# Four steps of an ordered f32 kernel on one core moved, and unread transpositions at three places

## The reference

```
def memory_attention(q, mk, mv):
    s = einsum('bshd,bmhd->bhsm', q, mk) * HEAD_DIM ** -0.5
    p = softmax(s, axis=-1)
    return einsum('bhsm,bmhd->bshd', p, mv)
...
for l in range(2):
    if l == 1:
        kv = rmsnorm(h, kv_norm) @ w_kv
        k_shared = rmsnorm(kv[..., :256], k_norm)        # per head of 64; the sliding keys
        v_shared = kv[..., 256:]
    proj = rmsnorm(h, norm_mix[l]) @ w_in[l]
    main, mq = proj[..., :768], proj[..., 768:]
    ...
    mkv = rmsnorm(mem, mem_norm[l]) @ w_mem_kv[l]
    mk = rmsnorm(mkv[..., :256], mem_k_norm[l])          # per head; the memory keys
    mv = mkv[..., 256:]
    mem_out = memory_attention(rmsnorm(mq, mem_q_norm[l]), mk, mv)
    h = h + concat(main_out, mem_out) @ w_out[l]
    h = h + sq_relu_mlp(rmsnorm(h, norm_mlp[l]), w_up[l], w_down[l])
```

## Time and profile before

| what | value |
|---|---|
| runs, us | 985.48, 986.09, 991.14; median 986.09 |
| the profiled execution, us | 986.21 |
| its span, us | 984.4 |
| TensorE busy | 976.6 us, 99%, 8662 instructions |
| VectorE busy | 692.8 us, 70% |
| ScalarE busy | 538.2 us, 55% |
| granted clock of TensorE | 1.00 |
| DMA | 168.97 MB, mean 172 GB/s |
| chain that ended last | PE 80%, DVE 12%, ACT 5%, issue 2%, DMA 1% |

### The profile page before, as it was taken

One profiled execution on the slowest core, in us unless ns is written; L12 is line 12 of the kernel. 1 busy time (PEld: TensorE's weight loads), 2 busy tenths in 40 slices (PEclk: granted clock), 3 DMA queues, 4 the chain that ended last, 5 costly groups with the idle time before them and its releaser, 6 DMA issues.

```text
span 984.4 us, 20641 instructions
## 1 busy us (share of the span) xinstructions
PE 976.6 (99%) x8662; PEld 948.6 (96%) x8662; DVE 692.8 (70%) x854; ACT 538.2 (55%) x688; POOL 38.7 (4%) x28
## 2 busy tenths in 40 slices
PE   9999999999999999999999999999999999999998
PEld 6999999999999999999989999999999999999998
DVE  5687765557789888999977655557777856555553
ACT  5657545546665455567645543445657755344432
POOL 0045230000000000000000000000000000000000
PEclk9999999999999999999999999999999999999999
DMA  7743433334644665453442755555553226655551
GB/s 280 253 172 132 160 102 122 130 129 172 246 171 172 214 213 180 164 212 129 171 172 87 256 175 209 202 181 175 172 179 117 71 103 216 215 206 174 183 201 43
DMA packets 24977, 168.97 MB, mean 172 GB/s; under 512 B 2768, under 2 KB 3536, under 8 KB 4944
## 3 DMA queue, kind: packets, MB, share of 16 engines
q1 hardware_dynamic: 24336, 165.82, 47.9%
q10 hardware_dynamic: 576, 2.20, 0.7%
HBM read 166.96 MB, written 1.05 MB: 171 GB/s over the span
## 4 chain that ended last, share of the span: by engine, by line
PE 80%; DVE 12%; ACT 5%; issue 2%; DMA 1%; DVEq 0%; SPq 0%; ACTq 0%
PE G L617 9%; PE G L611 8%; PE G L612 8%; PE D L606 7%; PE D L604 7%; PE D L605 7%; PE G L604 6%; PE G L605 6%; PE G L606 6%; DVE wlo L1922 5%; ACT whi L1404 2%; PE M L604 2%; PE M L606 2%; PE M L605 2%; PE M L909 1%
## 5 line engine op out<-in xcount | busy, mean ns | idle before, releaser
L1922 DVE TENSOR_TENSOR wlo<-raw,whi 128x2048 fp32r<-128x2048 f32 x155 | 354.9, 2295 | 114.8 <-ACT whi L1404 114.7
L1404 ACT ACTIVATE whi<-raw 128x2048 fp32r<-128x2048 f32 x155 | 295.5, 1909 | 59.0 <-PE D L606 46.2
L611 PE MATMUL G<-xh,whi 128*128 128x256 f32 x736 | 178.2, 286 | 0.0
L604 PE MATMUL D<-hh,whi 128*128 128x256 f32 x624 | 172.2, 276 | 0.0
L605 PE MATMUL D<-hl,whi 128*128 128x256 f32 x624 | 172.2, 276 | 0.0
L606 PE MATMUL D<-hh,wlo 128*128 128x256 f32 x624 | 172.2, 276 | 0.0
L612 PE MATMUL G<-xl,whi 128*128 128x256 f32 x736 | 172.2, 278 | 0.0
L611 PEld LDWEIGHTS G<-xh,whi 128*128 128x128 f32 x736 | 138.5, 188 | 4.5 <-issue 3.2
L612 PEld LDWEIGHTS G<-xl,whi 128*128 128x128 f32 x736 | 138.5, 188 | 1.3 <-issue 1.2
L604 PE MATMUL G<-xh,whi 128*128 128x256 f32 x448 | 123.9, 276 | 0.3 <-DVE wlo L1922 0.2
L605 PE MATMUL G<-xl,whi 128*128 128x256 f32 x448 | 123.7, 276 | 0.0
(11 more groups left out here) (450 smaller groups left out, 1643.7 us busy)
## 6 DMA issues: line engine op xcount, KB each, us to landing
raw<-wall_dram SPq DMA_DIRECT2D x155, 1024.0 KB, 4.9
x<-x_dram SPq DMA_DIRECT2D x4, 256.0 KB, 5.3
mem<-mem_dram ACTq DMA_DIRECT2D x1, 1024.0 KB, 4.8
poolw<-pool_w_dram ACTq DMA_DIRECT2D x1, 768.0 KB, 6.4
out_dram<-x SPq DMA_DIRECT2D x3, 256.0 KB, 2.2
cst<-cst_dram SPq DMA_DIRECT2D x1, 448.0 KB, 12.2
lora<-lora_dram SPq DMA_DIRECT2D x1, 256.0 KB, 11.7
sgw<-sg_w_dram SPq DMA_DIRECT2D x1, 256.0 KB, 12.4
```

Source lines behind the costliest of these rows:

```text
L604: mm(out, w_h, hi, start=start, stop=False, skip_group_check=skip)
L611: mm(out, w_h, hi, start=start, stop=False, skip_group_check=True)
L1404: signal(fn(whi[:, pan.slot, 0:w], raw[:, pan.slot, 0:w], ACT.Copy), "w_hi")
L1922: signal(tt(wlo[:, pan.slot, 0:w], raw[:, pan.slot, 0:w], f32(whi[:, pan.slot, 0:w]), SUB), "w_lo")
```

## The change

Four steps of the table move, each for some of the engines.

- `hn` is cut in two on TensorE's side (`hn_sum`): for the memory keys of layer 0 the sum stands ahead of the panel in0q. `hn_square` 0 stands ahead of mkv0's second panel, which for ScalarE means ahead of the copy of mv.
- the refinement of rstd becomes a step of its own (`late_root`) and stands behind the row sums in layer 0.
- VectorE reads ks in `score_m` 1, between the maxima and their correction; `root_s` 0 stands behind `hn_square` 2.
- in pair 1 of the gated net, second half, `more` stands ahead of the tap copies and of hh.

Two unread transpositions are added in the first panel of `wo` and behind the last part of `pv_s`, and two replace the four small products behind `rw_gates`.

```diff
-    W += [("panel", mkv + 1), ("hn_square", 0)] + sums[3]
-    W += [("panel", PAN["in0q"]), ("hn", 0), ("ahead_lo", PAN["in0q"]), ("begin", m0), ("square_m", 0), ("root", 3), ("sum_m", 0), ("score_m", 0), ("turn_mv", 0), ("panel", m0),
+    W += [("hn_square", 0), ("panel", mkv + 1)] + sums[3]
+    W += [("hn_sum", 0), ("panel", PAN["in0q"]), ("hn", 0), ("ahead_lo", PAN["in0q"]), ("begin", m0), ("square_m", 0), ("root", 3), ("sum_m", 0), ("late_root", 3), ("score_m", 0), ("turn_mv", 0), ("panel", m0),
...
-          ("panel", q1), ("turn_mv", 1), ("hn", 1), ...
+          ("panel", q1), ("turn_mv", 1), ("hn_sum", 1), ("hn", 1), ...
-          ("panel", q1 + 1), ("square_s", 0), ("ahead", k1), ("begin", k1), ("score_m", 1), ("sum_s", 0), ("root_s", 0), ("panel", k1),
-          ("begin", k1 + 1), ("hn_square", 2), ("exp_m", 1), ("soft_m", 1), ("hn", 2), ...
+          ("panel", q1 + 1), ("square_s", 0), ("ahead", k1), ("begin", k1), ("score_m", 1), ("sum_s", 0), ("panel", k1),
+          ("begin", k1 + 1), ("hn_square", 2), ("root_s", 0), ("exp_m", 1), ("soft_m", 1), ("hn_sum", 2), ("hn", 2), ...
@@ first_panel, TensorE @@
+                if count == XLN["wo"] and u == 0:
+                    free("M0")
+                    unread_turns(M[0], 2)
                 pe.wait_ge(S("xl"), count - 3 + u)
@@ rw_gates, TensorE @@
-            unread_few()
+            unread_turns(M[0], 2)
@@ pv_s, TensorE @@
+            if g == 2:
+                free("D1")
+                unread_turns(DB[1], 2)
@@ ffn, ScalarE @@
+                        if js == 1 and u:
+                            more(pan, 3)
                         act.wait_ge(S(f"up_read{f}"), 2 * j + u + 1)
...
-                        if not (u and isinstance(j, int) and j == ni - 1):
+                        if not (u and isinstance(j, int) and j in (1, ni - 1)):
                             more(pan, 3)
@@ root, VectorE @@
+            if n != 3:
+                late_root(n)
+
+        def late_root(n):
             dve.wait_ge(S("rs"), n + 1)
             newton(rstd[:], M[1][:, 0, :], D, 1e-6, rtmp[:], ("rs_read", n + 1))
@@ panel and score_m, VectorE @@
-            elif name == "kv":
+            elif name == "kv" and i:
                 read(p)
...
             own(ins)
+            if l:
+                read(PAN["kv"])
             row_newton(l, 0)
```

More of the change, by code:

```diff
@@ L413, in build @@
     W += [("panel", PAN["mkv1"]), ("hn_square", 1), ("panel", PAN["mkv1"] + 1), ("root", 5), ("parts5b",),
-          ("panel", q1), ("turn_mv", 1), ("hn", 1), ("square_m", 1), ("ahead", q1 + 1), ("begin", q1 + 1), ("sum_m", 1),
-          ("panel", q1 + 1), ("square_s", 0), ("ahead", k1), ("begin", k1), ("score_m", 1), ("sum_s", 0), ("root_s", 0), ("panel", k1),
-          ("begin", k1 + 1), ("hn_square", 2), ("exp_m", 1), ("soft_m", 1), ("hn", 2), ("ahead", k1 + 1), ("panel", k1 + 1),
+          ("panel", q1), ("turn_mv", 1), ("hn_sum", 1), ("hn", 1), ("square_m", 1), ("ahead", q1 + 1), ("begin", q1 + 1), ("sum_m", 1),
+          ("panel", q1 + 1), ("square_s", 0), ("ahead", k1), ("begin", k1), ("score_m", 1), ("sum_s", 0), ("panel", k1),
+          ("begin", k1 + 1), ("hn_square", 2), ("root_s", 0), ("exp_m", 1), ("soft_m", 1), ("hn_sum", 2), ("hn", 2), ("ahead", k1 + 1), ("panel", k1 + 1),
           ("begin", q2), ("ahead", q2), ("turn_p", 1), ("panel", q2), ("square_s", 1), ("turn_v",), ("score_s", 0),
@@ L686, in first_two, with unread_turns @@
                 ins.then_inc(S("pe_panel"), 1)
-        def unread_turns(bank):
-            for i in range(4):
+        def unread_turns(bank, n=4):
+            for i in range(n):
                 nc.tensor.transpose(bank[:, i // 2, i % 2 * P:(i % 2 + 1) * P], ident, ident)
-        def unread_few():
-            for _ in range(4):
-                mm(M[0][0:32, 0, 0:32], xh[:, 0, 0:32], xh[:, 0, 32:64], skip_group_check=True)
         def early_start():
@@ L1039, in rw_gn2 @@
             free("M0")
-            for i in range(2):
-                nc.tensor.transpose(M[0][:, 0, i * P:(i + 1) * P], ident, ident)
+            unread_turns(M[0], 2)
             freed.update({"D0": ("sb_out", 4), "D1": ("sb_arg", 4), "D2": ("rw_y", 1), "D3": ("rw_rs_read", 1)})
@@ L1361, in _ @@
                   "sg_turn": sg_turn, "sg_mix": sg_mix, "sb_turn": sb_turn, "sb_z": sb_z, "sb_q": sb_q,
-                  "sb_o": sb_o, "ffn": ffn, "mem_sum": mem_sum, "hn": hn, "turn_mv": turn_mv,
+                  "sb_o": sb_o, "ffn": ffn, "mem_sum": mem_sum, "hn_sum": hn, "turn_mv": turn_mv,
                   "turn_v": turn_v, "score_m": score_m, "turn_p": turn_p, "pv_m": pv_m, "pool_mm": pool_mm,
@@ L2567, in _ @@
         dve.wait_ge(S("ld_cst"), 16)
-        walk(dve, {"norm": norm, "root": root, "final_norm": final_norm, "pool": windows, "add_sq": add_sq, "add_mem": add_mem, "parts": parts, "parts5b": parts5b,
+        walk(dve, {"norm": norm, "root": root, "late_root": late_root, "final_norm": final_norm, "pool": windows, "add_sq": add_sq, "add_mem": add_mem, "parts": parts, "parts5b": parts5b,
                    "panel": panel, "rw_low": rw_low, "rw_gates": rw_gates, "rw_cum": rw_cum, "rw_key": rw_key, "rw_square": rw_square, "rw_scale": rw_scale,
```

## The result

The changed kernel takes 996.88 us (median of 6, 994.09 to 998.68) against 986.73 (6 runs) before: ratio 1.0102, interval [1.0083, 1.0120], slower by 10 us. The forecast was 988.4, the range ended at 991.4. The profiled execution took 994.09, the lowest of the six, with a span of 990.6 against 984.4, so the profile shows 6.2 us of the loss; the rest has to be found in other executions.

The account below looks back on a forecast made before the run. TensorE, busy 976.6 of 984.4 us, was taken to bound the kernel. 986.21 + 3.7 - 0.4 - 0.3 - 0.3 - 0.35 = 988.56, less 0.12, gave 988.4 us, range 986.6 to 991.4.

Parts of the forecast that it names:

- The pause: TensorE ahead of the early memory keys' sum: a new wait of 3.54 us, ended by ScalarE's squares; both edits there cost +3.7.
- hy began right behind mq: ScalarE at the memory keys: hy follows the copy of mq without waiting for the sum, 3.6 to 3.8 us later.
- The part that was to come back inside in0q: Panel in0q behind the memory keys' sum: waits inside it absorb 0.24 to 0.44 us of the lateness.
- The row sums: TensorE at 478.97: its 0.57 us wait goes, but TensorE waits for ml at wout0 instead; rival that the gain holds, 0.13.
- The sliding keys': TensorE at 740.65: the 0.57 us wait goes, part ends in a later VectorE wait; taken as -0.4 us.
- The clock: Rival, chance 0.15: TensorE's clock falls in the new wait, making in0q slower, for 990.8 or 993.1 us.
- the forecast's own sign of being wrong: Behind the memory keys' wait: the forecast is wrong if the granted clock falls there.
- the lower price: Clock rival with the first half of in0q at the slow rate: 2.35 us added, 990.8 us; rival's chance 0.15.
- The split of the gated stage: TensorE's wait at 303.58 for VectorE's split of a weight panel: earlier whi removes it, -0.3 us, bounds -0.41 and 0.
- The transpositions: Unread ones at rw_gates (-0.3), after the last sliding output (-0.35) and wo (0), quickening matmul pitch; rival of none, 0.08.
- the dearer case: At rw_gates: the stretch turns quick, gaining 0.58 us, but the next turns slow and loses the same; upper bound +0.63.
- The last place: Transpositions after the last output of the sliding attention: quicker matmuls behind, -0.35 us, bounds -0.35 and +0.14.

Follow-up runs that it names:

- e10: The change with the gated net's split edit taken back and ScalarE squaring the memory keys ahead of a split, shortening the pause: 989.25 us, ratio 1.0036.
- e12: The kernel before with the edit at the row sums alone: 986.94 us, ratio 1.0003.
- e11: The kernel before with the edit at the sliding keys alone: 986.01 us, ratio 0.9996.
- e9: The change without its edit at the gated net's split, memory keys' pause kept: 994.71 us, ratio 1.0076.
- e1: The change without its edit at the memory keys, sum behind in0q again: 991.63 us, ratio 1.0024.
- e3: The change with ScalarE squaring the memory keys right behind their copy, ahead of the first norm part: 991.86 us, ratio 1.0027.
- e4: The change with eight unread products on TensorE filling the pause ahead of the memory keys' sum: 998.82 us, ratio 1.0099.
- e6: The kernel before with the earlier split of the gated net alone: 990.75 us, ratio 1.0022.
- e8: The change without its memory keys edit, plus two unread transpositions right ahead of the gated net's loop: 988.00 us, ratio 1.0027.
- e5: The change without its edits at the memory keys and at the gated net's split: 986.87 us, ratio 0.9999.
- e2: The kernel before with the edit at the memory keys alone: 993.77 us, ratio 1.0057.

## Why the prediction was wrong

- **The pause** was right: place, releaser and length, 3.54 forecast and 3.37 of idle plus the 0.16 of the tail measured. hy began right behind mq, as forecast, 6.47 us late (477.25 instead of 470.78); without the clock's 2.55 that is 3.9, against 3.6 to 3.8. The part that was to come back inside in0q did not: in e10, at full clock, the sum and in0q took 6.62, where the forecast's terms make 6.2 to 6.4.
- **The row sums** were right: the wait went, and what was won there was waited out at the pool products and wout0 (e12).
- **The sliding keys'** term was too high for this execution: 0.57 was won at the sum and given back by 775, where the forecast kept 0.4; e11 alone kept 0.3.
- **The clock** is the first step that failed: the sum put its fall behind the new pause at nothing, and the forecast's own sign of being wrong, a granted clock that falls there, came. It stood among the rivals at 0.15, priced at 2.35 and more, with no row that could decide it. 20 of 24 executions of the kernels with such a pause show a lower mean. It cost 2.55 us in the profile, near the lower price; with it the forecast would have been 991.0, and the profile's span grew by 6.2, where the sum (988.56 against 986.21) and the 2.55 make 4.9. The Trainium skill's rule (TensorE: Matmul & The Clock Gate, HAM oscillation — how this bites in real kernels), that a long enough pause brings TensorE back to the lower clock, spoke for it. The windows of the change agree (0.50 behind 3.37 us of idle); in e9's profile the matmuls behind the pause began at 1.00 and the clock fell only after that.
- **The split of the gated stage** is the second, and about as large: "I take -0.3". The 0.36 came. But the forecast asked only which engine is late next, and not what the wait did for what stands behind it; a change of the loop's pitch had no term at all. Without the wait the loop is wide in 36 of 54 executions (e1, e3, e4, e6, e8; before, over all chips, 28 of 122), at some 5 us each. That the edit raises the share is shown by e5 and e6; that it does so through the lost wait is argued from the traces. The change's own profile has the narrow loop, so for its other executions this is argued from those kernels and from the times: 995.44 and 996.08 kept a mean clock of 1.000 and are still some 9 us above before, of which the pause without the clock makes some 4 (6.5 us of lateness at 520 in the profile, less 2.55).
- Behind that lies the reading of the earlier trace rows: two pitches seen in one execution were taken as belonging to places, to be bought for 0.5 us by a transposition. They vary from execution to execution, and over one loop of 1300 matmuls are worth more than any wait that the change took away. Of the runs shown (985.48, 986.09, 991.14) the highest belongs by its time to the other group; no trace of it is kept.
- **The transpositions** at rw_gates won 0.6 us in the profile and lost it in the next stretch, the dearer case that the forecast named but did not take (it took -0.3): 142 matmuls in the first window of the earlier trace rows instead of 138, then 133 where the kernel before has 138. That is no accident of this execution: the first stretch is narrow in 7 of 8 profiles with the transpositions and in 1 of 8 without, and in all 16 the stretch behind it has the other pitch. Before and after:

```profile
66.00:82.00 16.00, 16.00 (x138) 1.00 0.31 98
```

```profile
45.00:61.00 16.00, 16.00 (x142) 1.00 0.46 152
66.00:82.00 16.00, 16.00 (x133) 1.00 0.35 115
801.00:816.80 15.80, 15.80 (x142) 1.00 0.20 68
```

The last place did turn narrow (142 instead of 137) and kept 0.4 us; it is narrow in all 8 profiles with the transpositions, but in 3 of the 8 without them too.

In medians, though of different chips: 986.87 (e5, neither edit), 991.63 with the split (e1), 994.71 with the pause but not the split (e9), 996.88 with both. Pause and clock are 5 to 8 us, the split with its pitch 2 to 5, and they do not simply add, since the median of two groups jumps with their shares. Open: why the pitch is what it is at the start of a stretch; why the clock fell in some executions with the pause, for longer in some than in others, and not in the rest; why the share in the kernel before differs so between chips (2 of 29, 11 of 23); and why 3.5 us of the change's profiled execution lay outside its span, against 1.8 before.

## What to carry to other kernels

A pause of TensorE must be weighed by its length, not only by its sum: 3.4 us in one piece cost its own length and 1.5 to 2.5 us of low clock behind it in two profiles, 1.55 us left the clock alone. Before taking a wait away in front of a long dense loop, look at what the loop's pitch is in several executions, and judge by groups of runs rather than by a median. When a table moves a step on one engine, check on each other engine what the step still stands behind; an early sum is worth nothing while its reader waits for something else.

## What the runs showed of the hardware

- With the granted clock at 1.00, matmuls of 128x256 run through a whole loop at 113.1 or 117.6 ns (before, e1), and executions of one program differ in it. In each of the 16 profiles the gated net's loop has one of the two throughout.
- The granted clock fell to 0.50 within a pause of 3.4 us and stayed there for 5 to 6 us of renewed work in the change's profile; in e9's it fell more than 1 us behind such a pause and was back by 473, some 5 us behind it. It did not fall in e10's pause of 1.55 us, nor while TensorE did unread products (e4).
- A mean clock of 0.993 in two executions of e9 and one of e2, against 0.997 in the change's profile, says that it can be low for longer than the profiles show, or more than once; no trace here shows where.
